# Expert sum of a prompt tile: 64x64 diagonal blocks in two PSUM banks in place of 32x32 blocks in four

## What is computed

```python
def one_chunk(xc):                                   # 128 tokens
    qry = einsum('cd,dq->cq', xc, w_query)           # 8 heads, two halves
    sc = einsum('chpd,hpnd->chpn', qry, sub_keys)
    ...                                              # two rounds of top 16: 16 experts for each head
    g = softmax(best_s, axis=-1)
    u = expert_u[idx]; v = expert_v[idx]             # rows of 1024 numbers
    act = gelu(einsum('chkd,cd->chk', u, xc))
    return einsum('chk,chkd->cd', g * act, v)
```

## Time and profile before

| | us |
|---|---|
| median of 3 runs | 5404.61 |
| the profiled execution's own time | 5403.16 |
| its span, first to last instruction | 5400.8 |
| first and last copy of `acc` (L1483), ends of tiles 1 and 8 | 2845.5 and 5387.7 |
| one tile in between, (5387.7 - 2845.5) / 7 | 363.2 |
| mean granted TensorE clock | 0.729 of full speed |

### The profile page before, as it was taken

The page is one execution under the profiler, slowest core; times in us unless marked ns, Lnnn a source line. Parts: engine busy times, 40 slices in busy tenths (PEclk is TensorE's granted clock), DMA queues, the critical chain, the costliest instruction groups (busy, mean ns, idle before and its releaser), DMA issues.

```text
span 5400.8 us, 77300 instructions
## 1 busy us (share of the span) xinstructions
PE 3203.0 (59%) x27092; PEld 1852.2 (34%) x27092; DVE 3367.6 (62%) x7794; ACT 1035.3 (19%) x2743; POOL 1798.5 (33%) x1424
## 2 busy tenths in 40 slices
PE   8676487853888879974544535535445445355333
PEld 6436476642666654433211212212112122122000
DVE  4518666666777764657765756747647657567544
ACT  3310211102443431111111121121121111211111
POOL 0200122222424222322444434434434434444443
PEclk9887699985998999986656656656656556566555
DMA  5142577774333337766999989989989989899998
GB/s 204 52 169 83 179 302 285 301 288 137 113 131 128 117 143 301 277 227 271 388 389 365 385 339 389 387 347 385 382 341 388 379 345 391 337 394 387 377 404 340
DMA packets 270603, 1558.85 MB, mean 289 GB/s; under 512 B 27040, under 2 KB 37280, under 8 KB 102048
## 3 DMA queue, kind: packets, MB, share of 16 engines
q0 software_dynamic: 184320, 1342.26, 63.6%
q1 hardware_dynamic: 85920, 211.83, 10.6%
HBM read 1505.49 MB, written 48.50 MB: 288 GB/s over the span
## 4 chain that ended last, share of the span: by engine, by line
DMA 27%; issue 12%; PE 7%; DVE 5%; ACT 2%; POOL 2%; another core or an unknown queue 0%; DVEq 0%; POOLq 0%; ACTq 0%; SPq 0%
DMA prompt_exp_ring<-in_experts_dram,prompt_exp_idx 23%; PE prompt_exp_acc L1722 6%; DMA prompt_exp_ring<-in_experts_dram,prompt_exp_idx_all 3%; POOL prompt_exp_ring L1386 2%; DVE prompt_exp_junk L1627 2%; ACT prompt_exp_diag L1465 1%; PE prompt_exp_qp L1683 1%; PE prompt_exp_qp L1738 0%; DVE prompt_exp_best L1508 0%; DVE prompt_exp_pos L1512 0%; DVE prompt_exp_dot L1627 0%; ACT prompt_exp_ysq L1483 0%; DVE prompt_exp_crest L1517 0%; DVE prompt_exp_sel L1559 0%
## 5 line engine op out<-in xcount | busy, mean ns | idle before, releaser
L1722 PE MATMUL prompt_exp_acc<-prompt_exp_ring,prompt_exp_diag 32*32 32x512 f32 x16384 | 942.3, 949 | 1536.4 <-ACT prompt_exp_diag L1465 1504.1
L1627 DVE CUSTOM_DVE_ANT_0 prompt_exp_junk<-prompt_exp_ring,prompt_exp_h_now 128x1024 bf16<-128x1024 f32 x1024 | 1242.5, 1226 | 894.0 <-DMA prompt_exp_ring<-in_experts_dram,prompt_exp_idx 767.4
L1386 POOL DMA_INDIRECT prompt_exp_ring<-in_experts_dram,prompt_exp_idx x896 | 1072.0, 1196 | 1463.7 <-PE prompt_exp_acc L1722 1279.2
L1722 PEld LDWEIGHTS prompt_exp_acc<-prompt_exp_ring,prompt_exp_diag 32*32 32x32 f32 x16384 | 170.0, 128 | 2089.6 <-issue 2087.9
L1459 ACT ACTIVATE prompt_exp_ge<-prompt_exp_dot 128x2 f32<-128x2 f32 x512 | 104.1, 203 | 2415.9 <-DVE prompt_exp_dot L1627 2395.2
L169 DVE CUSTOM_DVE_ANT_0 bg_junk<-bg_ring,bg_h 128x1024 bf16<-128x1024 f32 x256 | 347.0, 1366 | 224.8 <-DMA bg_ring<-in_experts_dram,bg_idx 91.4
L144 POOL DMA_INDIRECT bg_ring<-in_experts_dram,bg_idx x128 | 150.9, 1179 | 717.4 <-DVE bg_acc L180 408.7
L1683 PEld LDWEIGHTS prompt_exp_qp<-prompt_exp_hT,prompt_exp_wq 128*128 128x128 f32 x2048 | 320.9, 247 | 150.7 <-issue 147.5
L180 DVE SCALAR_TENSOR_TENSOR bg_acc<-bg_ring,bg_w,bg_acc 128x1024 f32<-128x1024 f32 x256 | 346.0, 1352 | 9.1
L1683 PE MATMUL prompt_exp_qp<-prompt_exp_hT,prompt_exp_wq 128*128 128x128 f32 x2048 | 346.2, 338 | 5.7 <-issue 2.8
L144 POOL DMA_INDIRECT bg_ring<-in_experts_dram,bg_window x128 | 136.3, 1065 | 639.2 <-DVE bg_acc L180 606.0
(11 more groups left out here) (331 smaller groups left out, 5114.0 us busy)
## 6 DMA issues: line engine op xcount, KB each, us to landing
sample_proj_w<-in_w_all_dram SPq DMA_DIRECT2D x10, 2048.0 KB, 8.1
prompt_proj_w<-in_w_all_dram SPq DMA_DIRECT2D x10, 2048.0 KB
proj_dram<-prompt_proj_stage SPq DMA_DIRECT2D x80, 256.0 KB
prompt_exp_ring<-in_experts_dram,prompt_exp_idx POOLq DMA_INDIRECT x896
sample_exp_wq<-in_w_query_dram SPq DMA_DIRECT2D x4, 2048.0 KB, 18.3
prompt_att_q<-proj_dram SPq DMA_DIRECT2D x16, 512.0 KB, 8.5
mixed_dram<-prompt_att_OT SPq DMA_DIRECT2D x8, 1024.0 KB, 9.5
prompt_mrg_mixT<-mixed_dram SPq DMA_DIRECT2D x8, 1024.0 KB, 6.2
```

What stands on the lines that cost most here:

```text
L1386: nc.gpsimd.indirect_dma_start(out=ring[:, s % RING, :], out_offset=None, in_=experts, in_offset=bass.IndirectOffsetOnAxis(ap=column(s), a ...
L1627: nc.vector.tensor_tensor_reduce(out=junk[:, s % 2, :], in0=ring[:, s % RING, 0:D], in1=h_now[:], scale=1.0, scalar=0.0, op0=ALU.mult, op1 ...
L1722: last = nc.tensor.matmul(acc[at:at + Q, rows, :], diag[k, (g - 1) % 2, c, :], ring[k, s % RING, D + half * 512:D + half * 512 + 512], sta ...
```

## The change

`Q` becomes 64, so that the blocks are 64x64. A slot and a half of v now takes two matmuls, one for each block of 64 partitions. The PSUM tile `acc` has two banks in place of four. PSUM partitions 0 to 63 hold the left half of v and 64 to 127 the right half; both slots of a pair add into the same places, where before each slot of a pair had its own 32 partitions. The slots are now the outer loop and the halves the inner one. `diag` is 128x64 for a slot in place of 128x32. `parts` is half as large, and the unfolding multiplies two pieces for each half in place of four.

```diff
-Q = 32
+Q = 64
...
-        parts = ysq[:].rearrange("p a (b c) -> p (a b) c", c=512)
+        parts = ysq[:, 0, :].rearrange("p (b c) -> p b c", c=512)
...
-                            for half in range(2):
-                                for c in range(PAIR):
-                                    s = PAIR * (g - 1) + c
+                            for c in range(PAIR):
+                                s = PAIR * (g - 1) + c
+                                for half in range(2):
                                     for rows in range(NQ):
-                                        k, at = slice(Q * rows, Q * rows + Q), Q * (2 * half + c)
+                                        k, at = slice(Q * rows, Q * rows + Q), Q * half
                                         last = nc.tensor.matmul(acc[at:at + Q, rows, :], diag[k, (g - 1) % 2, c, :],
                                                                 ring[k, s % RING, D + half * 512:D + half * 512 + 512],
-                                                                start=(g == 1), stop=(g == STEPS))
+                                                                start=(s == 0), stop=(s == SLOTS - 1))
                             last.then_inc(used, 1)
...
-        unfold[2 * Q * half:2 * Q * (half + 1), half, :] = fold[:2 * Q]
+        unfold[Q * half:Q * (half + 1), half, :] = fold[:Q]
```

## The result

The changed kernel takes **5511.8 us** (median of 4 runs, 5502.7 to 5524.3), the kernel before beside it 5401.1: a ratio of 1.0208 with a 95% interval of 1.0189 to 1.0228. So it got slower by 2.1%, where 1.6% was forecast (5490 us); the time lies in the range of 5405 to 5610. The profiled execution has a span of 5505.0 us against 5400.8, 104 us more.

A forecast was written before the change was run, and what follows sets the result against it. The prediction took transfers as the bound where undisturbed, elsewhere the loop refilling the ring. Its terms, 5403.2 + 67 (tiles with top-16 work) + 5 (last tile) + 13 (restarts) + 2 (end), gave 5490 us, range 5405 to 5610.

The forecast's parts named there:

- The sum of four waves: Expert stage, v sum on TensorE: a pair's 16 records make four waves, 3.85 us at 1.2 GHz, +1.8 us.
- The mix of clocks: TensorE in the expert stage: half the sums at each clock level, mean 2.95 us, so +1.15 us a sum.
- The rule from the Trainium skill's page: V sum: about 60 cycles of overhead per matmul, so fewer records make the mixed +1.15 about +0.5; first term 30 us.
- The slack of 1.7 us: Ring refill loop: 18.4 us against 20.1 us for eight rows, leaving 1.7 us when nothing else goes on.
- The false term: Fetch part of the ring loop: 5.9 us from issue to dot, the pair's second row 2.5 us later.
- the term of the last tile: Last tile, low clock: 1.9 us of growth meets 1.7 of slack, 0.3 a cycle, +5 us (0 to 30).
- The term of the other seven: Seven tiles with top-16 work: half of 1.2 us in each of 16 cycles, +67 us (0 to 134).
- Restart, +13 us: Start of the next tile: nothing hides the first v sum, at the low clock, 7 x 1.9 = +13 us.
- A tile's end, 0 and +2 us: Last sums, acc copy and unfolding: covered at seven ends, cost nothing; at the very end nothing hides them, +2 us.
- The clock pays for it: Rival, chance 0.19: busier TensorE holds the upper clock, slack covers the middle, only restarts cost; 5412 us.
- Low clock, bound throughout: Rival, chance 0.16: all sums take 3.85 us and nothing is absorbed; 5661 us, with some slack left 5600.
- The blocks did run together: Opposite of a rival, chance 0.05: only two 64x64 blocks run at once, eight waves a sum, 5800 us or more.

The follow-up runs named there:

- b_twice: Kernel before (32x32 blocks) with each pair's sixteen matmuls issued a second time, giving four waves; 5582.0 us, ratio 1.0332.
- b_early: Kernel before with a pair's weights formed between the next pair's two dots, its diagonals ahead of the next Gelu; 5232.3 us, ratio 0.9695.
- a_early: Changed kernel (64x64 blocks) with a pair's weights formed between the next pair's dots, its diagonals ahead of the next Gelu; 5294.8 us, ratio 0.9816.
- b_early_delay: b_early plus the four extra scaled copies on ScalarE of b_delay; 5304.2 us, ratio 0.9845 to the kernel before.
- b_delay: Kernel before with four extra scaled copies on ScalarE ahead of each pair's diagonals, 1.07 us more in the loop; 5510.7 us, ratio 1.0208.
- b_slot: Kernel before with slots as the outer matmul loop and each slot's ring place given back by itself; 5329.4 us, ratio 0.9895.
- b_endcopy: Kernel before with ScalarE copying acc four times in place of once at each tile's end; 5415.4 us, ratio 1.0063.
- a_warm: Changed kernel with two spare matmuls behind each pair's sum into a free PSUM bank; 5411.6 us, ratio 1.0041 to the kernel before.

## Why the prediction was right, and where it was not

**The sum of four waves: right.** Forecast 3.7 to 4.1 us at the lower clock and 1.9 to 2.1 at the upper; it was 3.69 and 1.95. The four combinations of strips run together. The value taken, 3.85, was a little high: its nearest row, 4.07, is that of four waves in 64 records, as b_twice has them, and 16 take 0.4 us less.

**The mix of clocks: right.** Half and half was a guess, and a lucky one: 261 of the 512 sums took over 2.9 us. The mean was 2.81 where 2.95 was taken, with 0.70 and 0.76 of the clock in the stretches above. The rule from the Trainium skill's page TensorEngine Tiling (Array Packing), Instruction Overhead, would have halved the growth to +0.5 us; it was +0.97, and the trace sides with counting waves.

**The slack of 1.7 us: wrong, and this is the step that failed.** It came from a loop of 18.4 us against 20.1 us of transfer. But the last tile of before went at 401 GB/s, a cycle of 8.39 MB / 401 = 20.9 us. Had there been 1.7 us of slack, it would have gone at 417. b_early's last tile does (418), and a_early's and b_early_delay's, too. The false term is the fetch: 5.9 + 2.5 = 8.4 us for a pair was read from one fetch into an empty DMA at a tile's start. Measured over 52 pairs of the last tile of before, with other pairs under way, it is 10.6 us from GpSimd's first issue to the start of the pair's second dot. From there it is 7.3 us to the first matmul (7.0 in the prediction), 2.07 of sum, and 0.93 to the next issue: 20.9 in all. Nor did the fetch give way when the sum grew: it is 10.8 us in the kernel after. In b_early, where the transfers are the bound, it is 12.6, and there the rows do queue.

The prediction had both numbers, 20.9 and 18.4, and called the difference a disturbance. As a result, the term of the last tile was +5 us where the cycle grew from 20.9 to 8.39 / 376 = 22.3, so 16 x 1.4 = +22. The term of the other seven took half of 1.2 us, and nearly all of the growth came: in the mean of all eight tiles a turn got **1.01 us** longer for 0.97 + 0.05 us of longer loop, 0.88 for 1.07 in b_delay, 1.42 for 1.43 in b_twice. (Without each tile's first turn, which holds the restart, it is 1.10, 0.93 and 1.39.) The 120 turns of the trace cost 121 us, where the prediction had 72 for its 128.

**Restart, +13 us: wrong.** The first sum of a tile took 1.3 to 1.7 us longer, and GpSimd's issue behind it came later by nearly as much, but VectorE's first dot on a fresh row, its ninth, came only 0.1 to 0.9 us later: 3.2 us over the seven restarts. From the timeline of the kernel after at one tile's start, as in the earlier trace rows:

```profile
4384.27 0.69 DVE L1617 COPY prompt_exp_h_now<-prompt_exp_h_next 128x1024 f32<-128x1024 f32 x1 [9.68 <-issue]
...
4396.95 0.93 POOL L1386 DMA_INDIRECT prompt_exp_ring<-in_experts_dram,prompt_exp_idx  x1 [22.58 <-PE prompt_exp_acc L1722]
...
4402.64 1.22 DVE L1627 CUSTOM_DVE_ANT_0 prompt_exp_junk<-prompt_exp_ring,prompt_exp_h_now 128x1024 bf16<-128x1024 f32 x1 [5.78 <-DMA prompt_exp_ring<-in_experts_dram,prompt_exp_idx]
```

GpSimd's issue comes 12.7 us behind VectorE's start in place of 11.4. It takes 0.93 us where the one of before took 1.93, and the dot comes at 18.4 us where it came at 18.3. At all seven restarts that issue took 0.93 or 0.94 us after and 1.80 or 1.93 before. This microsecond was the cover, and it wasn't named. In b_slot the same issue, at 11.2 us, takes 0.94 us, and the dot comes at 16.8. Why the issue is shorter is open.

**A tile's end, 0 and +2 us: wrong sign.** From the last dot of a tile to the addition of the residual, before and after (VectorE's timeline, at the tile of the earlier trace rows and its like):

```profile
4305.42 1.23 DVE L1627 CUSTOM_DVE_ANT_0 prompt_exp_junk<-prompt_exp_ring,prompt_exp_h_now 128x1024 bf16<-128x1024 f32 x1 [1.05 <-DMA prompt_exp_ring<-in_experts_dram,prompt_exp_idx]
...
4317.23 1.22 DVE L1656 TENSOR_TENSOR prompt_exp_ysq<-prompt_exp_qp,prompt_exp_xr 128x1024 f32<-128x1024 f32 x1 [10.14 <-PE prompt_exp_qp L1738]
```
```profile
4373.37 1.22 DVE L1656 TENSOR_TENSOR prompt_exp_ysq<-prompt_exp_qp,prompt_exp_xr 128x1024 f32<-128x1024 f32 x1 [7.46 <-PE prompt_exp_qp L1738]
```

VectorE is idle for 10.14 us before and for 7.46 after. Over the first seven ends this distance, from the last dot to the addition, sums to 90.8 us before and 72.0 after, 18.8 less. The doubled sums cost nothing there: from the last dot to the start of the copy it is even 1.9 us less over the seven. At the end shown, as at three others, the last two sums ran back to back at the upper clock in 3.66 us, where two took 4.37 here and 4.07 at the last end; at the other four ends they took 5.1 to 6.2. The copy took 0.85 us less, as forecast, 6.0 over seven. The largest part, 10.7 us, is the unfolding, which the prediction took as equal. Its records in both kernels (ns of one: shortest, median, longest):

```profile
L1738 PE MATMUL prompt_exp_qp<-prompt_exp_ysq,prompt_exp_unfold x128: 589/1061/1062, 2847.5 to 5391.1; 128*32 128x512 f32 x128
```
```profile
L1738 PE MATMUL prompt_exp_qp<-prompt_exp_ysq,prompt_exp_unfold x64: 592/592/644, 2862.3 to 5495.7; 128*64 128x512 f32 x64
```

Before, the unfolding took 3.64 us at six of the eight ends and 2.4 or 2.5 at two; after, it took 1.94 at all of them. The granted clock in it was 0.50 before at the ends with 3.64 us, 0.74 and 0.78 at the two shorter ones, and 1.00 at every end after. So the work is about equal, as forecast (3.64 us at half the clock), and the clock is what the term lacked: behind the longer sums the end of a tile ran at the upper level. VectorE's wait at the five jumps got a little longer, 49.0 us for 45.6 in all, and moved forward with the end. b_endcopy shows that it can give way to a later end; why it didn't lengthen enough to swallow an earlier one isn't shown. The parts add up: 18.8 less, 3.4 more at the jumps and 3.2 more at the restarts are 12.2 less from a tile's last dot to the next one's ninth, as measured.

**The sum.** Too small in the loop, by 49 us, and too large at the ends and restarts, by some 30. The forecast was 17 us under the profiled execution and 22 under the median: nearer than its terms, because their errors have opposite signs, which is luck.

**The rivals.** "The clock pays for it" didn't come, but a_warm shows that its mechanism is right: with the clock held up, the loss is 0.4%, where the rival had 0.2% (5412 us). That the times, 5411.6 and 5412, agree to a microsecond is chance, for the before beside a_warm is 5386.5 us, and of the rival's 13 us of restart 4.5 came. The point against it held too: in the kernel itself the clock doesn't stay up, and half of the sums are long. "Low clock, bound throughout" was half right, bound throughout without the low clock. The blocks did run together.

## What to carry to other kernels

In a ring that is refilled when its last reader is done, add up the loop from rows of the running state, and compare the sum with the period that the trace shows. If the period is longer than the transfer time, there is no slack, and each microsecond put anywhere in the loop, also on an engine that idles more than four fifths of the time (ScalarE: 33 us busy of 270 in the last tile of before), comes back once per turn (here 0.88 to 1.42 us for 1.07 to 1.43). The remedy is in the loop as well: form the weights before the next row comes, and give each place back by itself, which turned a change that cost 2.1% into the base of a kernel 3.9% faster than before. With the old blocks the same two edits give 3.4%. And at a place where an engine has just been busier, ask for the clock of what runs next: here it shortened the unfolding.

## What the runs showed of the hardware

- Four 64x64 tiles of the array run together as sixteen 32x32 tiles do: 16 records of 512 fp32 columns in 3.69 us at 1.2 GHz and 1.95 us at 2.4, against 32 records in 2.02 and 1.15.
- Sixty-four records of 32x32 blocks took 3.27 us in the mean where sixteen of 64x64 took 2.81, both being four waves: 4.08 against 3.69 at the lower clock, and 2.34 to 2.76 against 1.95 at the upper.
- Spare matmuls behind each sum kept TensorE near the upper clock in a_warm. With TensorE busy for 208 of 270 us, the clock was 0.96, and the DMA moved 400 GB/s, as with 107 us of TensorE at clock 0.50.
- 418 to 420 GB/s was the most that the fetches of 8 KB rows reached over 270 us, in five kernels alike.
- The first of these fetches into an empty DMA took 5.9 us from its issue to its dot, which gives an estimated 8.4 us for a pair with the second row 2.5 us behind. With other pairs under way a pair took 10.6 us in the mean.
